# Mean squares of the second block's heads: the block of ones becomes the weights, the squares stream through in four groups of 32 output rows, and four transpositions bring the result back

## The reference

```python
def rmsnorm(x, g):
    xf = x.astype(jnp.float32)
    y = xf * lax.rsqrt(jnp.mean(xf * xf, axis=-1, keepdims=True) + EPS)
    return (y * g.astype(jnp.float32)).astype(x.dtype)

for l in range(DEPTH):
    h = rmsnorm(x, norm1[l])
    p = h @ w_in[l]
    ...
    q = rope(rmsnorm(q, q_norm[l]))
    k = rope(rmsnorm(k, k_norm[l]))
    y_a = windowed_gqa(q, k, v, sink[l])
```

## Time and profile before

| what | value |
|---|---|
| three runs | 1778.01, 1780.29, 1781.07 us; median 1780.29 |
| profiled execution | 1775.64 us, of which the span from the first to the last instruction is 1773.6 us |
| PE busy | 1698.6 us (96% of the span), 8858 matmuls |
| DVE, ACT, POOL busy | 779.4, 695.1, 677.5 us |
| mean granted TensorE clock | 0.978 |

### The profile page before, as it was taken

The page is one execution under the profiler, slowest core; times in us unless marked ns, Lnnn a source line. Parts: engine busy times, 40 slices in busy tenths (PEclk is TensorE's granted clock), DMA queues, the critical chain, the costliest instruction groups (busy, mean ns, idle before and its releaser), DMA issues.

```text
span 1773.6 us, 24207 instructions
## 1 busy us (share of the span) xinstructions
PE 1698.6 (96%) x8858; PEld 1336.3 (75%) x8858; DVE 779.4 (44%) x1496; ACT 695.1 (39%) x1144; POOL 677.5 (38%) x523
## 2 busy tenths in 40 slices
PE   6999999999999979989999999999998999999999
PEld 5876568787666857867888888878776888888887
DVE  7226564402656264674455115532565365403540
ACT  4444462534445152554343224333354344313431
POOL 3432215443311642425443444345152534434443
PEclk9999999999999979989999999999898999999999
DMA  7320103222110211212222232222121222232222
GB/s 255 106 72 28 69 25 120 96 96 72 49 49 25 84 48 48 73 49 81 101 95 85 89 104 95 82 98 96 49 73 49 95 95 95 74 116 96 95 78 88
DMA packets 24608, 145.90 MB, mean 82 GB/s; under 512 B 3152, under 2 KB 3536, under 8 KB 10704
## 3 DMA queue, kind: packets, MB, share of 16 engines
q1 hardware_dynamic: 21840, 138.01, 22.7%
q10 hardware_dynamic: 2688, 6.82, 1.0%
HBM read 142.72 MB, written 2.10 MB: 82 GB/s over the span
## 4 chain that ended last, share of the span: by engine, by line
PE 68%; issue 19%; POOL 7%; DVE 3%; ACT 2%; DMA 1%; POOLq 0%; ACTq 0%; DVEq 0%
PE ring L520 59%; POOL w_lo L506 7%; PE outs L580 2%; PE scores L566 1%; PE ring L566 1%; PE scores L590 1%; PE ring L604 1%; PE ring L590 1%; PE ring L660 1%; DMA xt<-in_x 1%; PE ring L922 1%; PE ring L634 1%; DVE g L1737 0%; ACT xh L1253 0%; ACT xt L1249 0%
## 5 line engine op out<-in xcount | busy, mean ns | idle before, releaser
L506 POOL TENSOR_TENSOR w_lo<-w_stage,w_hi 128x258 fp32r<-128x258 f32 (+5 forms) x471 | 643.9, 1397 | 1053.0 <-ACT w_hi L1026 652.2
L520 PE MATMUL ring<-xh,w_lo 128*128 128x512 f32 x1296 | 518.0, 400 | 25.0 <-DVE w_lo L1444 10.6
L520 PE MATMUL ring<-xh,w_hi 128*128 128x512 f32 x1296 | 511.9, 395 | 0.0
L520 PE MATMUL ring<-xl,w_hi 128*128 128x512 f32 x1296 | 511.6, 395 | 0.0
L520 PEld LDWEIGHTS ring<-xh,w_lo 128*128 128x128 f32 x1296 | 244.9, 189 | 87.2 <-DVE w_lo L1444 10.6
L520 PEld LDWEIGHTS ring<-xh,w_hi 128*128 128x128 f32 x1296 | 244.8, 189 | 55.4
L520 PEld LDWEIGHTS ring<-xl,w_hi 128*128 128x128 f32 x1296 | 245.2, 189 | 53.0
L1375 ACT ACTIVATE w_hi<-w_stage 128x2048 fp32r<-128x2048 f32 (+2 forms) x70 | 116.6, 1666 | 158.8 <-PE ring L520 158.8
L1385 ACT ACTIVATE g<-ring,convw 128x512 f32<-128x512 f32 x88 | 68.1, 778 | 245.4 <-DVE ring L1876 245.4
L1026 ACT ACTIVATE w_hi<-w_stage 128x2064 fp32r<-128x2064 f32 (+2 forms) x81 | 123.5, 1537 | 92.7 <-PE ring L520 92.1
L1858 DVE TENSOR_TENSOR xt<-xt,ring 128x512 f32<-128x512 f32 x48 | 33.0, 688 | 248.2 <-PE ring L520 248.2
(11 more groups left out here) (288 smaller groups left out, 2255.8 us busy)
## 6 DMA issues: line engine op xcount, KB each, us to landing
w_stage<-in_mixed SPq DMA_DIRECT2D x62, 1032.0 KB, 4.8
w_stage<-in_up SPq DMA_DIRECT2D x44, 1024.0 KB, 4.8
w_stage<-in_down SPq DMA_DIRECT2D x16, 768.0 KB, 4.2
w_stage<-in_down SPq DMA_DIRECT2D x16, 640.0 KB, 3.9
xt<-in_x ACTq DMA_DIRECT2D x4, 512.0 KB, 11.3
out_t<-xt ACTq DMA_DIRECT2D x8, 256.0 KB, 2.0
mem_f<-in_mem SPq DMA_DIRECT2D x1, 1024.0 KB, 9.5
bias_r<-in_relb SPq DMA_DIRECT2D x1, 1024.0 KB, 11.5
```

The costliest lines, as they stand in the source:

```text
L506: ins = nc.gpsimd.tensor_tensor(w_lo[:, slot, cols], source[:, cols], w_hi[:, slot, cols].bitcast(F32), ALU.subtract)
L520: ins = nc.tensor.matmul(o, lhs, rhs, start=start, stop=stop, skip_group_check=True)
```

## The change

`hms` is made the other way round: a piece of `head_ones` with 32 columns (two of them 1/64, the rest zero) is the weights, and each tile of squares streams through as 512 columns. Tile t writes the 32 output rows from 32 (t mod 4); tile 4 is added to the rows of tile 0 with its ones two columns further. So five products take the place of twenty. The result is head by token. ACT copies the bank to `probs`, and PE transposes it in four pieces to a new place in the ring, `("hmt", l)`, between the rotations of q tiles 1 and 2. DVE reads `hmt` after the rope of tile 0, with two instructions in place of one. `head_ones` is now 128 x 40; it leaves the constants loaded at the start and is loaded by ACT behind the two tables for the second block.

```diff
-        take(("tv2", l), ("hms", l), *[("rq", l, t) for t in range(4)], ("u", l, 0, 0), ("rq", l, 4), ("u", l, 1, 0), ("k_bc", l))
+        take(("tv2", l), ("hms", l), ("rq", l, 0), ("rq", l, 1), ("hmt", l), ("rq", l, 2), ("rq", l, 3), ("u", l, 0, 0), ("rq", l, 4), ("u", l, 1, 0), ("k_bc", l))
...
+        head_ones = place("head_ones", [P, 40], F32, union + 25 * TOK * 4)
...
-                for t in range(5):
-                    x = head_sq(t)
+                pe.wait_ge(S("tables_loaded"), 48)
+                for t in (0, 1, 2, 3, 4):
+                    g0 = 32 * (t % 4)
+                    ins = nc.tensor.matmul(o[g0:g0 + 32, :], head_ones[:, 2:34] if t < 4 else head_ones[:, 0:32], head_sq(t),
+                                           start=(t < 4), stop=(t > 0), skip_group_check=True)
+                ins.then_inc(S("ring_full"), 1)
+
+                def head_columns():
+
+                    wait_taken(pe, ("hms", l))
+                    o = acquire(("hmt", l))
                     for j in range(TT):
-                        ins = nc.tensor.matmul(o[:, 8 * t + 2 * j:8 * t + 2 * j + 2], x[:, j * P:j * P + P], head_ones[:, :],
-                                               start=(t == 0 and j == 0), stop=True, skip_group_check=True)
-                ins.then_inc(S("ring_full"), 1)
+                        ins = nc.tensor.transpose(o[:, j * P:j * P + P], probs[:, 0, j * P:j * P + P], ident[:, :])
+                    ins.then_inc(S("ring_full"), 1)
 
                 for t in range(4):
                     wait_taken(pe, ("q", l, t))
                     rotate(("rq", l, t), rot64, q2[:, t, :])
+                    if t == 1:
+                        head_columns()
...
+                    load(head_ones[:, :], dram["head_ones"], "tables_loaded")
...
+                evac(("hms", l), probs[:, 0, :])
                 act.wait_ge(S("head_ms"), l + 1)
...
-                name = ("hms", l)
-                wait_full(dve, name)
-                step(v.tensor_tensor(rtok[:, 4:8], rtok[:, 0:4], rtok[:, 0:4], ALU.mult))
-                inv2 = rtok[:, 4:8].unsqueeze(1).unsqueeze(3).to_broadcast([P, 5, TT, 2])
-                v.tensor_tensor(head_inv[:, :, :, :], bank(name)[:, 0:40].rearrange("p (t j h) -> p t j h", t=5, j=TT), inv2,
-                                ALU.mult).then_inc(freed(name), 1)
-                wait_taken(dve, name)
-                dve.sem_inc(S("head_ms"), 1)
...
                     rope(("rq", l, t), x, full, cos64, sin64, [x], "rope2_done")
+                    if t == 0:
+                        name = ("hmt", l)
+                        step(v.tensor_tensor(rtok[:, 4:8], rtok[:, 0:4], rtok[:, 0:4], ALU.mult))
+                        wait_full(dve, name)
+                        cells = bank(name)[:, :].rearrange("p (j t c) -> p t j c", j=TT, t=4)
+                        step(v.tensor_tensor(head_inv[:, 0:4, :, :], cells[:, :, :, 0:2],
+                                             rtok[:, 4:8].unsqueeze(1).unsqueeze(3).to_broadcast([P, 4, TT, 2]), ALU.mult))
+                        v.tensor_tensor(head_inv[:, 4, :, :], cells[:, 0, :, 2:4], rtok[:, 4:8].unsqueeze(2).to_broadcast([P, TT, 2]),
+                                        ALU.mult).then_inc(freed(name), 1)
+                        wait_taken(dve, name)
+                        dve.sem_inc(S("head_ms"), 1)
```

More of the change, by code:

```diff
@@ L275, in build @@
         ones = place("ones", [P, 1], F32)
-        head_ones = place("head_ones", [P, 2], F32)
         rot64 = place("rot64", [P, P], F32)
@@ L464, in load_constants @@
                 sp.dma_start(pos_i[:, :], bass.AP(dram["pos"].tensor, 0, [[0, P], [1, TOK]])).then_inc(S("pos_loaded"), 16)
-                for dst, key in ((ident, "ident"), (ones, "ones"), (head_ones, "head_ones"), (rot64, "rot64"), (rot32, "rot32")):
+                for dst, key in ((ident, "ident"), (ones, "ones"), (rot64, "rot64"), (rot32, "rot32")):
                     sp.dma_start(dst[:, :], dram[key]).then_inc(S("const_loaded"), 16)
@@ L860, in _ @@
                             proj(("w", l, W_IN_TILES[2 * s + t]), (c0 + s) % 2, t, i, 1)
-                pe.wait_ge(S("const_loaded"), 16 * 7)
+                pe.wait_ge(S("const_loaded"), 16 * 6)
                 for t in range(2):
@@ L1117, in _ @@
                     act.wait_ge(S("vec_loaded"), 16)
-                    act.wait_ge(S("const_loaded"), 16 * 7)
+                    act.wait_ge(S("const_loaded"), 16 * 6)
                     rotary_tables()
@@ L1477, in _ @@
                 v.tensor_scalar(r, r, lim, -lim, ALU.min, ALU.max).then_inc(S("angles"), 1)
-            dve.wait_ge(S("const_loaded"), 16 * 7)
+            dve.wait_ge(S("const_loaded"), 16 * 6)
             dve.wait_ge(S("sines"), 4)
@@ L1744, in _ @@
                 norm_inv(2 * l)
-                dve.wait_ge(S("tables_loaded"), 32)
+                dve.wait_ge(S("tables_loaded"), 48)
                 for t in range(5):
@@ L2008, in layouts @@
     f["ones"] = np.full((P, 1), 1.0 / DM, np.float32)
-    f["head_ones"] = np.kron(np.eye(2), np.full((HD, 1), 1.0 / HD)).astype(np.float32)
+    f["head_ones"] = np.pad(np.kron(np.eye(2), np.full((HD, 1), 1.0 / HD)), ((0, 0), (2, 36))).astype(np.float32)
     def rotation(n):
```

## The result

The changed kernel's median was 1766.89 us (four runs, 1762.2 to 1769.07) against 1779.74 us for the kernel before (four runs); the ratio is 0.9925, 95% interval 0.9901 to 0.9949. Faster, as forecast, but by 12.9 us instead of 10.2, and just outside the range (1766.9 where its lower end was 1767). Two later comparisons on other occasions gave 0.9927 (0.9909 to 0.9946) and 0.9894 (0.9877 to 0.9911).

What follows compares the result with a forecast made beforehand. PE was taken as the bound, busy 96% of the span. Gains of 4.3 and 6.1 us, plus 0.2, minus 0.4, sum to 10.2 us: 1780.3 to 1770.1 us, range 1767 to 1778.

Steps and rivals of the forecast that it cites:

- The stretch: First weight load of the mean squares to DVE's product with k: 4.3 and 6.1 us gained in the two layers.
- Block: Mean squares on PE: ten instructions, four groups at once, take 1.8 us where 5.65 stood in layer 0.
- wait of the u tile: PE idles 0.8 us before the first u tile, until DVE's rope frees the second q rotation's bank.
- product with k: DVE's product with k comes 14.7 us after the mean squares' first load, before 19.00 and 20.82.
- staircase: Rival: the mean squares' ten instructions take six units, 2.6 us; gain 8.5 us, 1771.8; chance 0.18.
- one after another: Rival: the ten instructions do not overlap, at full clock; 2.6 us more a layer, gain 5.0, 1775.3; chance 0.08.
- the falling clock: Rival: groups overlap but the clock still falls in mean squares and rotations; gain 3.2 us, 1777.1; chance 0.11.
- That DVE's and PE's sides meet: Before DVE's product with k, both engines' chains end at 14.5 us; 14.7 with hand-overs.
- The first scores: Product with k to the next u tile takes 2.3 us in both layers: 0.2 gained, 0.4 lost.
- The start of the block: Times counted from the mean squares' first weight load, with no term for a later start.
- The rest costs nothing: Loading `head_ones` behind the sine table, more than 80 us before PE needs it, adds 0 us.
- The case of a larger gain: Whole run: a gain larger than the forecast's 10.2 us, outside the range; chance 0.03.

Runs made afterwards that it cites:

- The experiment with full width: Changed kernel with its five products over all 128 output rows, in no column groups: 1769.42 us, ratio 0.9942.
- the old products: Changed kernel's DVE order with the old twenty two-column products, no copy and no transpositions: 1773.63 us, ratio 0.9972.
- the changed kernel's second profile: Profile from a repeat of the changed kernel with no edit: median 1768.33 us over six runs, ratio 0.9927.

## Why the prediction was right and wrong

*The stretch* was right in nearly every term. Block 1.83 us (forecast 1.8); rope's start 3.06 (2.9); wait of the u tile 0.70 (0.8); product with k 14.57 in both layers (14.7); gain 4.4 and 6.2 us (4.3 and 6.1). The experiment with full width showed the price of the groups, and the old products brought the lower clock back. Of the rivals, staircase, one after another and the falling clock are refuted for this kernel by the profile. The staircase took each product's two halves to stand next to each other; in the trace the first halves of tiles 0 to 3 start within 0.02 us, then the second halves, and in this order they also end, so that matmuls in order make no staircase. The Trainium skill, page TensorE: Matmul & The Clock Gate, section Part 3: Packing small matmuls, gives 2.38 times for three groups of 32 rows; here four products, eight units if one after another (3.44 us), took two: tile 4 starts at 693.25, 0.88 us after tile 0, a factor of 3.9. So the trace, with four groups, shows more than the page's figure for three.

*That DVE's and PE's sides meet* was half right: DVE ended last by itself, as reading behind tile 1 showed: PE's wait shrank by 0.66 us and the stretch stayed.

*The first scores* were sized at 0.2 gained and 0.4 lost. In layer 0 the u tile behind them starts 2.40 us after the product with k (706.94 to 709.34; before 2.50), in layer 1 also 2.40 (before 1.89): 0.1 gained, 0.5 lost.

*The start of the block* was taken to be the same. It comes 0.2 us later behind the transposition of v than before (0.59 against 0.39), so 0.4 us of the 10.7 are no gain of the run.

*The step that failed* is "The rest costs nothing". I weighed the loading of `head_ones` only as a load. Its leaving the constants moved every tensor behind it by 32 bytes, and that is worth some 3 us in each layer of the second block. Between the stretches 540.96 us with the shift undone and 537.63 in the kernel that reads behind tile 1, both with 6.8 us at the lower clock: 3.3. Behind them 508.76 against 505.83 in the changed kernel's second profile, both with 10.2: 2.9. In sum about 6.3 us, which no term of the forecast had. The case of a larger gain had a chance of 0.03 and no mechanism.

Stretch 10.7, later start -0.4, scores -0.4 and address 6.3 make 16.2 us. The medians over all runs differ by 14.2, those of the first comparison by 12.9. One loss is seen: behind the stretches the changed kernel took 505.83 us with 10.2 at the lower clock, against 504.22 with 10.6 in before with `head_ones` moved. Of these 1.6 us the scores explain 0.5; what costs the other 1.1 stays open. That leaves 0.9 us, which the scatter of the runs covers (1759.87 to 1769.07 for the changed kernel).

A clock that falls more often is not what is missing. The mean granted clock is 0.974 over the 41 executions of before in the later comparisons, and 0.978 over the 14 of the changed kernel. That is some 93 and 77 us at the lower clock, and the two stretches, with 17 us of it before and none now, make up the difference. Whether the changed kernel meets the lower clock more often in the one stage ahead of the stretch stays open: the three profiles have 692.4, 693.7 and 688.3 us there, the two of before 684.2 and 693.6, too few to tell.

That the measured gain still lay within 3 us of the forecast is luck: 6.3 us came that it had not seen, and losses that it had not seen either, with the scatter, took more than half of them back in the first comparison.

## What to carry to other kernels

A product whose moving side has two columns is nearly all weight loads; turned round, with the small matrix as weights and the outputs in separate groups of 32 rows, it runs dense, keeps the clock, and lets several products share the array: 5.65 us became 1.83. Follow every tensor that a diff removes or adds through the memory map: what lies behind it moves, and a dense product over a moved tensor can change its pace. When executions of one kernel differ by 10 us because of the clock in an untouched stage, compare stage by stage between two fixed instructions, and then add up all the stages: the two rotations moved ahead gained 2.2 us in their stretches and kept 1.0 to 1.9 of them to the end.

## What the runs showed of the hardware

Matmuls of 128 x 512 fp32r operands ran at 233 ns each when the streamed tensor started 32 bytes above a multiple of 64, and at 228 ns when it started at a multiple of 64 (36 matmuls in 8.40 and 8.20 us), in the out-projection and down products. Two kernels had the first address (before, and the changed one with `union` 32 bytes on) and the slower pace, six the second and the faster, whichever way the address came about. The weights' addresses were the same. It was seen for shifts of 32 bytes alone. A multiple of 64 is not all that counts: `xh` and `xl` also start at one, by the sizes of the tensors ahead of them, and their matmuls ran at 231.0 ns in every kernel. Why is open.

Four fp32 products of 512 columns in four groups of 32 output rows took 0.88 us, one in full width 0.86 (two instructions of 0.43). With PE busy all the time on weight loads and products of two columns, the granted clock fell to its lower level for 6.8 and 10.2 us (before, both layers); with the dense products in the same place it stayed at 1.00.
